# First column group of a squared-ReLU perceptron with one level of block products, and the work around it reordered

## Chip, cores and metric

The kernel runs on one core of one Trainium2 chip. The metric is the device time of one launch in microseconds. All data are fp32; matrix products run on TensorE in fp32, each logical product as two matmul records in the trace.

## What is computed

Two network blocks follow each other on 1024 tokens of width 1024. The change touches the end of the second one: a layer norm, the perceptron with squared ReLU, and the last layer norm.

```python
h = layer_norm_2(ALPHA * h + cross_attention(h, memf, ...), ln2_g, ln2_b)
h = layer_norm_2(ALPHA * h + squared_relu_mlp(h, mlp_w1, mlp_w2), ln3_g, ln3_b)

def squared_relu_mlp(x, w1, w2):          # w1: 1024 x 4096, w2: 4096 x 1024
    hdn = jnp.square(jax.nn.relu(jnp.einsum('bld,df->blf', x, w1)))
    return jnp.einsum('blf,fd->bld', hdn, w2)
```

## The kernel before

Activations lie transposed, features on partitions, tokens in columns; the two halves of 512 tokens are normed one after the other. Norms are numbered: 2 and 3 are the halves of the second layer norm, 4 and 5 those of the third. A norm `n` takes its mean with a matmul by ones over a sum of eight rows (`add_r`, GpSimd), is centred (VectorE), squared (ScalarE), its squares summed (`add_sq` on GpSimd, three of eight on VectorE), and then has its root, its scaling and its shift.

**First product.** The hidden columns are cut into 8 quads of 512. Each quad is a product of a 1024x512 block of `w1` with all tokens, done with the seven products of the Strassen-Winograd scheme; `items` lists these (q, m1), 56 in all, in the order (0,1) (0,2) (1,1) (1,2), then 6 7 5 4 3 of quad 0, the same of quad 1, then quads 2 to 7 with `QUAD_ORDER` 1 2 6 7 5 4 3. The token side of product m1 is an operand (`OPERANDS`: B11, B21, B22 or the sums T1 to T4), made once in quad 0 by `operand`. The weight side is a raw block or one of the sums S1 to S4, made by GpSimd in `level_sums`. Each item is done by the same scheme again (a second level): seven passes of two products of 256 columns, whose weight sums s1 to s4 GpSimd makes (also `level_sums`, in a ring of three items) and whose token sums t1 to t4 come from `more_sums` (called as `more`). TensorE's order over the items is `PASSES`, in which passes 7 and 4 of an item fall into the next item's turn:

```python
PASSES = ((1, 0), (7, -1), (5, 0), (2, 0), (4, -1), (6, 0), (3, 0))
```

Blocks of an item are put together in PSUM and by three VectorE adds (`add_block`: c11, c12, c22) and four ScalarE copies (`copy`: t1, t5, t2, c21). Pass 4 waits for `c22`, pass 6 for `t1`, 3 for `t5`, 7 for `t2`. Then VectorE joins the seven products of a quad (`combine`: U2, C11, U3, U4, C22, C21, C12), squares the ReLU in one op (R11, R22, R21, R12: `max` with 0, then `mult` with itself), and forms the token operands of the second product (T3, T1, T2, T4), which SP stores to DRAM (`store_operand`).

**Second product.** `LastProduct`: 28 steps, seven products m1 in `LAST_ORDER` (5 6 1 7 4 2 3) times four groups g. For step n, `load` fetches the hidden operand and the raw weights, `chain_sum` (VectorE) makes S, `right_sums` (VectorE) and `left_sums` (GpSimd) make the second level's sums, and PE does seven passes of 256 columns. After the last group of an m1 `add_blocks` empties PSUM and `combine_late` joins (U2 to C11) and adds the residual (R22, R21, R11, R12).

Every engine runs its queue in program order, and each of these orders is written out by hand (`copies_order`, `blocks_in_order`, the loops at the end of each engine's block); a wait is a count on one semaphore per engine (`Marks`). Norm 3's steps lie between the first items, norm 4's in steps 25 and 26 of the second product, norm 5's after it.

## Time and profile before

| | |
|---|---|
| median of three runs | 3309.31 us (3306.61 to 3310.32) |
| profiled execution | 3313.49 us, span 3311.7 us |
| first product of the quads to the first of the second product | 2520.2 to 2917.0 us of the span |
| second product | 2917.0 to 3278.0 us |
| last norm and stores | 3278.0 to 3311.7 us |
| busy over the whole span: TensorE, VectorE, GpSimd, ScalarE | 3170.8, 1801.2, 1099.2, 714.4 us |
| mean granted clock of TensorE | 0.98 of 2.4 GHz |

Times in the rows are microseconds from the span's start. PE is TensorE, DVE VectorE, ACT ScalarE, POOL GpSimd, SPq the queue of SyncE. An x behind a row counts records; square brackets give the idle time ahead of the row and what ended it.

### The profile page before, as it was taken

To read this page: it belongs to the slowest core of one execution; us is meant where nothing else is said; L and a number is where in the kernel's file an instruction comes from. 1 tells how busy PE (TensorE), PEld (TensorE's weight loads), DVE (VectorE), ACT (ScalarE), POOL (GpSimd) and SP (SyncE) were. 2 spreads that over 40 slices of the span, in tenths; PEclk is the share of its full clock that TensorE was granted. 3 is DMA by queue.
4 is the path that set the end of the run, shared out by engine and by line. 5 is a ranking of instruction groups with operands and counts; after the bars stand their busy time and mean duration, and the time that the engine had idled before them with its cause. 6 is when DMAs were issued, how large, how long until landed. Compare 5 with 4: busy or idle time off the path is not lost.

```text
span 3311.7 us, 31339 instructions
## 1 busy us (share of the span) xinstructions
PE 3170.8 (96%) x11908; PEld 1854.2 (56%) x11908; DVE 1801.2 (54%) x2603; ACT 714.4 (22%) x1247; POOL 1099.2 (33%) x846
## 2 busy tenths in 40 slices
PE   8989998999999999999999999999998899989995
PEld 3446464864444444444444554544555688878884
DVE  2387976731544343434325654752126777786866
ACT  3333334321100101101212234212223122200002
POOL 0010130003433433331211000341016999945545
PEclk9999999999999999999999999999999899999997
DMA  4211101241111111120212211211112233375651
GB/s 136 73 42 39 51 30 51 79 151 51 39 42 48 38 38 51 44 70 32 83 64 78 64 52 51 77 51 64 51 64 76 83 135 139 119 282 196 217 181 72
DMA packets 185859, 273.72 MB, mean 83 GB/s; under 512 B 7664, under 2 KB 134128, under 8 KB 185200
## 3 DMA queue, kind: packets, MB, share of 16 engines
q1 hardware_dynamic: 185712, 271.72, 24.1%
q8 instruction: 97, 1.59, 0.2%
q14 instruction: 50, 0.41, 0.0%
HBM read 231.85 MB, written 39.85 MB: 82 GB/s over the span
## 4 chain that ended last, share of the span: by engine, by line
PE 83%; DVE 9%; POOL 3%; issue 2%; ACT 2%; DMA 1%; SPq 0%; DVEq 0%; POOLq 0%; ACTq 0%
PE psum L1795 22%; PE psum L181 10%; PE psum L3421 8%; PE psum L3237 8%; PE psum L2320 8%; PE psum L402 7%; PE psum L1836 3%; PE psum L3937 3%; PE psum L1824 2%; DVE arena L1337 2%; DVE arena L1335 2%; PE psum L555 1%; POOL arena L4429 1%; PE psum L3914 1%; PE psum L3875 1%
## 5 line engine op out<-in xcount | busy, mean ns | idle before, releaser
L1795 PE MATMUL psum<-arena 128*128 128x512 f32 x1736 | 746.4, 592 | 1.9 <-DVE arena L2099 1.9
L1795 PEld LDWEIGHTS psum<-arena 128*128 128x128 f32 x1736 | 329.4, 190 | 417.2 <-issue 412.1
L2022 DVE TENSOR_TENSOR arena<-arena,psum 128x512 f32<-128x512 f32 x336 | 221.4, 686 | 458.5 <-PE psum L1795 275.4
L3421 PE MATMUL psum<-arena 128*128 128x256 f32 x1568 | 343.5, 382 | 3.3 <-DVE arena L3458 2.9
L402 PE MATMUL psum<-arena 128*128 128x512 f32 x768 | 336.9, 598 | 4.9 <-DVE arena L1193 4.9
L285 POOL TENSOR_TENSOR arena<-arena 128x512 f32<-128x512 f32 (+1 forms) x190 | 221.4, 1198 | 348.9 <-DMA arena<-w_ffn_gate 165.0
L181 PE MATMUL psum<-arena 128*128 128x512 f32 x768 | 332.4, 592 | 1.5 <-ACT arena L4095 1.5
L3237 PE MATMUL psum<-arena 128*128 128x256 f32 x1244 | 293.9, 390 | 38.3 <-DVE arena L3261 22.8
L3421 PEld LDWEIGHTS psum<-arena 128*128 128x128 f32 x1568 | 300.4, 192 | 46.9 <-issue 4.3
L3237 PEld LDWEIGHTS psum<-arena 128*128 128x128 f32 x1244 | 240.7, 195 | 81.5 <-DVE arena L3261 29.5
L402 PEld LDWEIGHTS psum<-arena 128*128 128x128 f32 x768 | 146.4, 192 | 188.7 <-issue 186.9
L2320 PE MATMUL psum<-arena 128*128 128x512 f32 x576 | 251.4, 595 | 0.0
L181 PEld LDWEIGHTS psum<-arena 128*128 128x128 f32 x768 | 145.8, 190 | 182.1 <-issue 180.6
L2320 PEld LDWEIGHTS psum<-arena 128*128 128x128 f32 x576 | 108.9, 191 | 136.4 <-issue 136.4
L4305 DVE TENSOR_TENSOR arena<-arena 128x1024 f32<-128x1024 f32 x88 | 152.9, 1738 | 0.4
L4429 POOL TENSOR_TENSOR arena<-arena 128x512 f32<-128x512 f32 x75 | 103.6, 1382 | 114.0 <-DVE arena L4179 73.0
L1943 ACT ACTIVATE arena<-psum 128x512 f32<-128x512 f32 x22 | 13.1, 597 | 536.6 <-PE psum L1795 536.6
L3141 POOL TENSOR_TENSOR arena<-small_sb,consts_sb 128x512 f32<-128x512 f32 x16 | 16.2, 1041 | 324.3 <-PE psum L2398 169.6
L2140 POOL TENSOR_TENSOR arena<-arena 128x512 f32<-128x512 f32 x42 | 53.1, 1264 | 194.8 <-ACT arena L1925 194.6
L1836 PE MATMUL psum<-arena 128*128 128x512 f32 x256 | 112.5, 592 | 0.0
L3937 PE MATMUL psum<-arena 128*128 128x512 f32 x224 | 97.0, 593 | 0.9 <-DVEq L241 0.9
L3439 POOL TENSOR_TENSOR arena<-arena 128x512 f32<-128x512 f32 x28 | 42.2, 1509 | 157.5 <-PE psum L3421 54.9
(529 smaller groups left out, 4179.0 us busy)
## 6 DMA issues: line engine op xcount, KB each, us to landing
arena<-w_in SPq DMA_DIRECT2D x42, 1024.0 KB, 5.3
arena<-mlp_w SPq DMA_DIRECT2D x72, 512.0 KB, 6.8
arena<-mlp_w SPq DMA_DIRECT2D x8, 2048.0 KB, 9.2
mlp_hidden_T<-arena SPq DMA_DIRECT2D x32, 512.0 KB, 2.6
arena<-mlp_hidden_T SPq DMA_DIRECT2D x16, 1024.0 KB, 6.0
arena<-w_out SPq DMA_DIRECT2D x12, 1024.0 KB, 5.0
mlp_hidden_B<-arena SPq DMA_DIRECT2D x24, 512.0 KB, 2.7
arena<-mlp_hidden_B SPq DMA_DIRECT2D x12, 1024.0 KB, 5.3
```

The lines of the kernel that those rows point to most:

```text
L181: mm = nc.tensor.matmul(self.out(i, x.shape[1]), part, x, start=(kk == 0), stop=(kk == self.kt - 1))
L285: return g.tensor_tensor(to[:, 0:kn, :], block_of(*a), block_of(*b), op)
L402: mm = nc.tensor.matmul(ps, slot(u)[:, k, m * P:(m + 1) * P], hn(k, h), start=(k == 0), stop=(k == KD - 1))
L1795: mm = nc.tensor.matmul(ps, left, right, start=(k == 0), stop=(k == kn - 1))
L1836: mm = nc.tensor.matmul(ps, raw(v)[:, k, m * P:(m + 1) * P], half_of(env, N0, k, h), start=(k == 0), stop=(k == KD - 1))
L2022: return v_.tensor_tensor(dst, dst, tiles.ps(*key), op)
L2320: mm = nc.tensor.matmul(ps, slot(n)[:, k, m * P:(m + 1) * P], x_half(k, h), start=(k == 0), stop=(k == KD - 1))
L3237: mm = self.env.nc.tensor.matmul(self.ps(n, m), left[:, k, :], right[:, k, :], start=(m in (1, 5, 2) and k == 0), stop=(k == 1), skip_grou ...
L3421: mm = self.env.nc.tensor.matmul(ps[:, 256 * r:256 * r + 256], left[:, s, r * P:(r + 1) * P], right[:, s, :], start=(first and s == 0 and ...
L3937: mm = nc.tensor.matmul(ps, left, mix_right[m](k), start=(k == 0), stop=(k == 3))
L4305: blocks.mark(v_.tensor_tensor(to, one, two, op), name, q)
L4429: fin(pool, nc.gpsimd.tensor_tensor(dst, dst, src, ALU.add), sem, value)
```

## The change

- The seven items of quad 0 are done with one level only: two passes `p0` and `p1` of four products of 512 columns each (`plain_product`), copied out of PSUM by ScalarE (`plain_copy`); no s1 to s4 for them. `passes` puts them between the passes of the two-level items.
- Squared ReLU of the first product moves from VectorE to ScalarE, as a Relu and, after it, a Square, both in place (`squared_relu`), one item later in the order.
- Orders: token sums (`more`) are made later and wait for the last pass of quad 0's item of the same operand; norm 3's rows are taken in another order and its steps sit at other items; on GpSimd `level_sums` runs for items 4, 5, 2, 3, 8, then 9 and on.
- Loads of the second product are split: `load_hidden` and `load_weights`; the weights of step 0 come after quad 6, the hidden operands of steps 0 and 1 before quad 7's `B22` store.
- `chain_sum(0)` goes from behind to ahead of `c22` of item 54, `right_sums(0)` between `c11` and `c12` of item 55, `right_sums(1)` ahead of `chain_sum(1)`.
- Norm sums: `R11` and `R12` come earlier and `C11` after `chain_sum(25)`; `add_r(4)` runs in two parts; `add_r(5)` sums the rows without `F_`, and TensorE adds the four rows of `F_` to the mean itself.

```diff
-def passes(items):
-
-    return [(n + d, m) for n in range(items + 1) for m, d in PASSES if 0 <= n + d < items]
+def passes(items, plain):
+
+    order = []
+    for n in range(items + 1):
+        if n in plain:
+            slots = ((7, -1), ("p0", 0), (4, -1), ("p1", 0))
+        else:
+            slots = PASSES
+        order += [(n + d, m) for m, d in slots if 0 <= n + d < items and (n + d in plain) == (m in ("p0", "p1"))]
+    return order
...
+        self.plain = {n for n, (q, m1) in enumerate(items) if q == 0}
...
+    def plain_product(self, pe, n, m):
+        q, m1 = self.items[n]
+        left, right, rt = self.weights(q, m1), self.x_of(OPERANDS[m1]), int(m == "p1")
+        if m == "p0":
+            if m1 == 1:
+                pe.wait_ge(*self.raw_in(q))
+            elif m1 in (3, 5, 6, 7):
+                self.summed.wait(pe, f"S{ {5: 1, 6: 2, 7: 3, 3: 4}[m1]}", q)
+        self.wait_bank(pe, n, m)
+        b = self.bank_of(n, m)
+        for k in range(4):
+            if m == "p0" and k % 2 == 0:
+                self.need_x(pe, OPERANDS[m1], 1 if k == 0 else 2)
+            mm = self.env.nc.tensor.matmul(self.env.ps(b * BANK, (b + 1) * BANK), left[:, k, rt * P:(rt + 1) * P], right[:, k, :], start=(k == 0),
+                                           stop=(k == 3), skip_group_check=True)
+        self.made.mark(mm, n, m)
+
+    def plain_copy(self, act, n, m):
+        q, m1 = self.items[n]
+        self.made.wait(act, n, m)
+        if m1 == 4:
+            self.blocks.wait(act, "C11", q)
+        b = self.bank_of(n, m)
+        to = self.out(q, m1)[:, int(m == "p1"), :]
+        self.copied.mark(self.env.nc.scalar.activation(to, self.env.ps(b * BANK, (b + 1) * BANK), ACT.Copy), m, n)
...
+            if q:
+                self.made.wait(pool, self.number[q, 6], 4)
...
-    order_in = lambda n: (4, 5, 6, 7, 0, 1, 2, 3) if n == 3 else range(8)
+    order_in = lambda n: (4, 5, 0, 1, 6, 7, 2, 3) if n == 3 else range(8)
...
-        combined = {6: ("U2", "C11", "R11"), 7: ("U3",), 5: ("U4", "C22", "R22"), 4: ("C21", "R21"), 3: ("C12", "R12")}
+        combined = {6: ("U2", "C11"), 7: ("U3",), 5: ("U4", "C22"), 4: ("C21",), 3: ("C12",)}
...
+        first_part = lambda n: 0 if n == 9 else 1
+        late_combined = {5: (), 6: (), 1: ("U2",), 7: ("U3", "U4", "C22", "R22"), 4: ("C21", "R21", "R11"), 2: (), 3: ()}
...
+        sums_first = (4, 5, 2, 3, 8)
+        more_after = {10: "T4", 11: "B22"}
...
+                    pe.wait_ge(scaled, 40)
                 ps = mean(n) if n else early.open(pe, "mean", n)
-                mm = nc.tensor.matmul(ps, env.const["ones"], acc_r(n), start=True, stop=True)
+                mm = nc.tensor.matmul(ps, env.const["ones"], acc_r(n), start=True, stop=(n != 5))
+                if n == 5:
+                    for i in range(4):
+                        blocks.wait(pe, "late", ("d12", "d21")[i // 2], 3)
+                        mm = nc.tensor.matmul(ps, env.const["ones"], F_[:, i, :], start=False, stop=(i == 3))
...
-                    late.load(sp, 0, before_late_load)
+                    late.load_hidden(sp, 0, before_late_load)
+                    late.load_hidden(sp, 1, before_late_load)
                 store_operand("B22", "R22", q)
                 if q == QUADS - 1:
-                    late.load(sp, 1, before_late_load)
-                    late.load(sp, 2, before_late_load)
+                    late.load_weights(sp, 1, before_late_load)
+                    late.load_hidden(sp, 2, before_late_load)
+                    late.load_weights(sp, 2, before_late_load)
                 store_operand("B21", "R21", q)
                 if q + 2 < QUADS:
-                    made.wait(sp, at_item[q, 4], 4)
+                    made.wait(sp, *quads.last_pass(at_item[q, 4]))
                     summed.wait(sp, "S4", q)
                     load_quad(q + 2)
+                elif q + 2 == QUADS:
+                    late.load_weights(sp, 0, before_late_load)
...
+            def squared_relu(n):
+                for name, q in activated_after(n):
+                    to = {"R11": a_[q % 2], "R22": e_, "R21": d_, "R12": c_[q % 2]}[name]
+                    blocks.wait(act, "C" + name[1:], q)
+                    copied.mark(nc.scalar.activation(to, to, ACT.Relu), "relu", name, q)
+                    copied.wait(act, "relu", name, q)
+                    copied.mark(nc.scalar.activation(to, to, ACT.Square), "square", name, q)
+
             for n in range(LAST_N + 1):
+                if n in quads.plain:
+                    quads.plain_copy(act, n, "p0")
+                    if n == 0:
+                        squares(3, range(4))
+                    quads.plain_copy(act, n, "p1")
+                    if n == 0:
+                        squares(3, range(4, 8))
+                    elif n == 1:
+                        std(3)
+                    if two_level(n - 1):
+                        quads.copy(act, n - 1, "c21")
+                    squared_relu(n - 2)
+                    continue
+                if n == 10:
+                    squared_relu(n - 2)
                 if n < LAST_N:
                     quads.copy(act, n, "t1")
-                if n == 1:
-                    squares(3, range(4))
-                if n < LAST_N:
                     quads.copy(act, n, "t5")
-                if n == 2:
-                    std(3)
-                elif n == 3:
-                    shifts(3, range(4))
-                if n:
+                if n == 3:
+                    shifts(3, range(4, 8))
+                if n != 10:
+                    squared_relu(n - 2)
+                if two_level(n - 1):
                     quads.copy(act, n - 1, "c21")
-                if n == 1:
-                    squares(3, range(4, 8))
-                elif n == 3:
-                    shifts(3, range(4, 8))
                 if n < LAST_N:
                     quads.copy(act, n, "t2")
+                if n == 2:
+                    shifts(3, range(4))
+            squared_relu(LAST_N - 1)
...
-                    dve.wait_ge(h_ready, 32)
+                    dve.wait_ge(h_ready, 24 + 4 + 4 * p)
...
+            centre(3)
             for n in range(LAST_N + 1):
-                if n:
+                if two_level(n - 1):
                     quads.add_block(dve, n - 1, "c22")
-                if n == 1:
-                    centre(3, range(4, 8))
-                elif n == LAST_N - 1:
-                    late.chain_sum(dve, 0)
-                elif n == LAST_N:
-                    late.right_sums(dve, 0)
-                    prepare(1)
-                for name, q in combined_after(n - 2)[1:]:
-                    combine(name, q)
-                if n < LAST_N:
-                    quads.add_block(dve, n, "c11")
-                    if n == 2:
-                        invert(3)
-                    elif n == 3:
-                        scale_rows(3, order_in(3)[4:8])
-                    quads.add_block(dve, n, "c12")
-                for name, q in combined_after(n - 1)[:1]:
-                    combine(name, q)
-                if n == 0:
-                    centre(3, range(4))
-                elif n == 2:
-                    scale_rows(3, order_in(3)[0:4])
-                elif n == 3:
+                if n == 3:
                     for p in range(2):
                         operand("T3", p)
                         operand("T2", p)
-                        if p == 0:
-                            operand("T4", p)
+                elif n == 4:
+                    for name in ("T4", "T1"):
+                        for p in range(2):
+                            operand(name, p)
+                elif n == 2:
+                    invert(3)
+                    scale_rows(3, order_in(3)[0:4])
+                for name, q in combined_after(n - 2)[first_part(n - 2):]:
+                    combine(name, q)
...
+                if two_level(n):
+                    quads.add_block(dve, n, "c11")
+                    if n == 2:
+                        scale_rows(3, order_in(3)[4:8])
+                    elif n == LAST_N - 1:
+                        late.right_sums(dve, 0)
+                    quads.add_block(dve, n, "c12")
+                for name, q in combined_after(n - 1)[:first_part(n - 1)]:
+                    combine(name, q)
+                if n == 5:
                     more("T2")
-                elif n == 4:
-                    operand("T1", 0)
-                    operand("T1", 1)
+                elif n == 7:
                     more("T1")
-                    operand("T4", 1)
-            for name, q in combined_after(LAST_N - 1)[1:]:
-                combine(name, q)
+                elif n == LAST_N - 2:
+                    late.chain_sum(dve, 0)
+            late.right_sums(dve, 1)
+            late.chain_sum(dve, 1)
...
-                    prepare(n + 2)
+                    late.chain_sum(dve, n + 2)
+                    if n == 23:
+                        combine_late("C11")
+                    late.right_sums(dve, n + 2)
                 if g == 3:
                     for name in late_combined[m1]:
                         combine_late(name)
+                elif n == 22:
+                    combine_late("R12")
+            blocks.wait(dve, "late", "C12", 1)
...
+                made.wait(pool, *quads.last_pass(at_item[0, {"T3": 7, "T4": 4, "B22": 3}[o]]))
...
-            quads.level_sums(pool, 0)
             pool.wait_ge(pv_done, 16)
-            quads.level_sums(pool, 1)
+            quads.level_sums(pool, 4)
+            quads.level_sums(pool, 5)
             add_r(3, range(5, 8))
             quads.level_sums(pool, 2)
             add_sq(3)
-            for n in range(3, LAST_N):
+            quads.level_sums(pool, 3)
+            quads.level_sums(pool, 8)
+            more("T3")
+            for n in range(9, LAST_N):
                 quads.level_sums(pool, n)
-                if n in (4, 6, 7):
-                    more({4: "T3", 6: "T4", 7: "B22"}[n])
-            for n in range(26):
+                if n in more_after:
+                    more(more_after[n])
+            for n in range(LATE):
+                if n == 26:
+                    add_r(4, range(4))
+                elif n == 27:
+                    add_sq(4)
                 late.left_sums(pool, n)
-            add_r(4, (4, 5, 6, 7, 0, 1, 2, 3))
-            late.left_sums(pool, 26)
-            add_sq(4)
-            late.left_sums(pool, 27)
+                if n == 22:
+                    add_r(4, range(4, 8))
```

## Rows read from the trace of the kernel before

**Rows 1.** Windows of the second half: length, busy (x) by engine, PEclk, DMA share, GB/s

```profile
2520.20:2645.20 125.00, 98.84 (x412) 82.06 (x411) 89.58 (x102) 30.29 (x72) 105.29 (x81) 0.88 0.18 68
2645.20:2901.30 256.10, 250.66 (x1149) 217.17 (x1148) 192.88 (x210) 63.00 (x164) 250.03 (x185) 1.00 0.36 134
2901.30:2917.00 15.70, 8.98 (x38) 7.38 (x37) 12.06 (x12) 1.53 (x4) 7.66 (x4) 0.84 0.50 179
...
3234.60:3278.00 43.40, 33.61 (x154) 28.30 (x154) 32.05 (x36) 10.75 (x18) 29.27 (x22) 0.92 0.13 49
3278.00:3311.70 33.70, 7.71 (x27) 5.77 (x26) 15.28 (x22) 10.27 (x17) 11.58 (x9) 0.54 0.17 62
```

**Rows 2.** What line 3237 (TensorE) waited for: us in all, waits

```profile
  DVE arena L3261: 52.3, 32
```

**Rows 3.** Timeline of TensorE: start, length, work xcount [idle before]

```profile
2404.52 13.90 PE L181 MATMUL psum<-arena 128*128 128x512 f32 x32
...
2607.46 3.78 PE L3237 MATMUL psum<-arena 128*128 128x256 f32 x8 [4.95 <-POOL arena L3280]
...
2640.85 6.21 PE L3237 MATMUL psum<-arena 128*128 128x256 f32 x28
```

**Rows 4.** Groups by line and shape: busy, mean ns | idle before

```profile
L1958 ACT ACTIVATE arena<-arena 128x1024 f32<-128x1024 f32 x22 | 21.9, 1048 | 0.0
...
L1943 ACT ACTIVATE arena<-psum 128x512 f32<-128x512 f32 x22 | 13.1, 597 | 536.6 <-PE psum L1795 536.6
...
L3247 ACT ACTIVATE conformer<-psum 128x256 f32<-128x256 f32 x112 | 43.1, 384 | 183.0 <-PE psum L3237 181.7 <-DVE arena L3261 1.3
...
L4088 ACT ACT_TABLE_LOAD x2 | 2.6, 1283 | 0.0
...
L4299 DVE SCALAR_TENSOR_TENSOR arena<-arena 128x1024 f32<-128x1024 f32 x32 | 52.7, 1648 | 0.6
...
L292 PE MATMUL psum<-consts_sb,arena 128*128 128x1 f32 x16 | 1.8, 245 | 0.0
```

**Rows 5.** Timeline of GpSimd, VectorE and TensorE about one collision, quad 3

```profile
2719.09 2.34 POOL L3287 TENSOR_TENSOR arena<-arena 128x1024 f32<-128x1024 f32 x1
2721.51 1.60 POOL L3292 TENSOR_TENSOR consts_sb<-arena 128x256 f32<-128x256 f32 x1
2723.07 0.72 POOL L3293 TENSOR_TENSOR consts_sb<-arena 128x256 f32<-128x256 f32 x1
...
2719.71 2.80 DVE L4305 TENSOR_TENSOR arena<-arena 128x1024 f32<-128x1024 f32 x1
...
2722.90 2.43 PE L3237 MATMUL psum<-arena 128*128 128x256 f32 x10 [0.33 <-DVE arena L3261]
```

**Rows 6.** Timeline of VectorE and TensorE at the change to the second product

```profile
2901.93 1.22 DVE L4305 TENSOR_TENSOR arena<-arena 128x1024 f32<-128x1024 f32 x1
...
2906.89 2.29 DVE L3458 TENSOR_TENSOR arena<-arena 128x2048 f32<-128x2048 f32 x1 [3.14 <-DMA arena<-mlp_w]
...
2916.32 1.75 DVE L3480 TENSOR_TENSOR arena<-arena 128x512 f32<-128x512 f32 x1
...
2915.11 2.07 PE L3237 MATMUL psum<-arena 128*128 128x256 f32 x4 [6.72 <-DVE arena L3261]
```

**Rows 7.** Timeline of GpSimd and TensorE, last steps and closing norm

```profile
3226.24 16.40 POOL L4429 TENSOR_TENSOR arena<-arena 128x512 f32<-128x512 f32 x7
...
3278.43 6.14 POOL L4429 TENSOR_TENSOR arena<-arena 128x512 f32<-128x512 f32 x4 [9.79 <-DVE arena L4354]
...
3242.70 2.08 PE L3828 MATMUL psum<-arena,consts_sb 128*128 128x512 f32 x2 [8.11 <-POOL arena L4429]
3244.57 11.55 PE L3421 MATMUL psum<-arena 128*128 128x256 f32 x48
...
3263.05 1.16 PE L299 MATMUL psum<-consts_sb,small_sb 128*128 128x128 f32 x8 [1.69 <-DVE small_sb L4208]
...
3284.62 2.07 PE L3828 MATMUL psum<-arena,consts_sb 128*128 128x512 f32 x2 [6.61 <-POOL arena L4429]
```

196 lines of the change are left out of this document (120 added, 76 removed).

## Prediction

> **What bounds the kernel now.** I read the windows of the second half first [rows 1]. Columns after the stretch are its length, then busy time of each engine. TensorE is the chain nearly everywhere; what can be won is where its length exceeds its busy time. Five stretches matter. The first fourteen items of the perceptron's quads take 125.0 us with TensorE busy 98.84 and a granted clock of 0.88. The following 41 items take 256.1 at full clock, GpSimd busy 250.03. The change-over to the second product takes 15.7 with 8.98 busy. The last four steps and their norm take 43.4 with 33.61 busy. The closing norm takes 33.7, almost without TensorE.
>
> Who kept TensorE waiting in the quads: above all the block adds of VectorE (line 3261), 52.3 us in 32 waits [rows 2]. In the first items the gaps are long enough for the clock to fall: after 4.95 us of waiting, eight records took 3.78, while 28 in a stretch took 6.21 [rows 3]. A logical product is two records. With the last record 0.38 long, a record of 256 columns steps by (6.21-0.38)/27 = 0.216; one of 512 columns by (13.90-0.59)/31 = 0.429 [rows 3]. So a pass (two products) of the two-level scheme is 0.864, an item of seven passes 6.05, and an item done plainly (8 products of 512 columns) 16 x 0.429 = 6.87. Each plain item thus costs 0.82 more TensorE work, 5.7 us over seven. The question is how much waiting goes with it.
>
> **First fourteen items.** Work left: seven plain items 48.1; 47 passes of the other items up to pass 3 of item 13, 40.6; the statistics 1.8 [rows 4], about 1.2 [rows 7] and two records of 512 columns, 0.86: 3.8. Together 92.5 us. Now the queues, in us from the stage's start.
> Items 0 and 1 need only `B11` and `B21`, which are there; they fill 0 to 14.7 and hide the norm: mean after 4.3, VectorE's eight centring steps, ScalarE's squares and GpSimd's five sums end near 14. Items 2 and 3 run to about 33, waiting 0.7 for `c22` of item 2 behind the row scaling. `T3` and `T2` (four 128x1024 sums, 1.22 each alone [rows 6]) follow on VectorE from 25.7 to 30.7; item 4 needs the second half of `T2` at 30.9. `T4` and `T1` end by 38, item 6 needs `T1` at 44. Items 4 to 8 need no level sums and are copied by ScalarE (0.60 each [rows 4]) under 3.4 us passes: no wait up to 64.6. So TensorE stays at full clock where it now drops. The moved buffers cost nothing: the same ops on other addresses. Nor do the norm's rows in another order, which let the first halves of `T3` and `T2` start after four shifts; otherwise item 4 would wait some 3 us more.
> Behind that the trouble is moved, not gone. GpSimd's `more("T3")` now waits for item 5's last pass, 43.9, and from there it has eleven blocks of sums to make for items 9 to 13, 36.3 us at the undisturbed 0.72 per 256 columns and 2.34 per 1024 [rows 5]. VectorE's fifteen combinations fall into the same time, and the two hold each other up: an op of 256 columns takes 1.60 beside them [rows 5]. With an idle 1.8 and about 12 of such waits, `S4` of quad 1 is ready near 94, and TensorE wants it near 91.5. On ScalarE, `R22` and `R21` of quad 0 stand ahead of `t1` and `t2` of item 9 (1.3 lost over two items); on VectorE the four operands of quad 0 wait for `R12` and delay `c22` of item 10 (1.5); `U2` and `C11` share one iteration, then `R11` delays `t2` of item 11 (2.5); `s12` is late by about 3.4; 1.0 for the smaller ones. With the 0.7 that is 10: end at 102.5 instead of 125.0, **gain 22.5**. Without GpSimd's and VectorE's mutual waits it would be 97 (28 gained), with full ones 110 (15 gained).
>
> **Squared ReLU on ScalarE, quads 2 to 7.** VectorE loses four ops of 1.648 per quad; ScalarE gains eight. No Relu runs in this half; the nearest row is an in-place 128x1024 activation of 1.048 [rows 4]. With the wait between the steps I take 2.2 per pair (bounds 2.1 and, if each step pays a further copy-sized 0.38, 2.9). ScalarE is 63.0 busy of 256.1, so it fits; what counts is its order. In a period the second combination is ready about 3.5 to 4.4 after the period's start, its pair ends at 5.7 to 6.6, then `c21` and `t2` (0.384 each) end at 6.5 to 7.4, and TensorE wants `t2` at 6.91. Two such periods per quad (`R11`, `R22`), a loss of 0 to 0.5 each. Waiting on ScalarE's pair are also SP's stores and, through `R12`, VectorE's `T3`; both have a period's slack here.
> Against it: these 41 items lose 256.1 - 41 x 6.05 = 8 us now, mostly where a combination stands in GpSimd's way: 2.80 instead of 1.22 beside a weight sum of 2.34, and `c22` behind it stops TensorE for 0.33 [rows 5, 6]. Four fewer such ops per quad give GpSimd some 4 us back, so its weight sums move earlier. I take 3.5 of the 8 back: **gain 3.5** (bounds -5 and +6).
> The Trainium skill speaks against this part (ScalarE: Activation LUTs, Rules for kernel authors): relu and mul belong on VectorE, not ScalarE. By the rows a pair is dearer by about 0.5 us; were all 32 pairs on the path, as the rule would have it, 16 us were lost and the time near 3289. That is the first rival below; no run yet shows which engine's time counts.
>
> **Change-over.** Now `chain_sum(0)` stands behind `c22` of item 54 and waits for weights until 2906.89; TensorE waits 6.72 and runs its next four records in 2.07 [rows 6]. The early `load_weights(0)` removes that wait (the copy is issued a quad earlier and hidden by it). But the sum (2.29 [rows 6]) now stands ahead of `c22` of item 54, which comes at 4.45 of its period instead of 3.46: 1.0 lost. Then `right_sums(0)` stands ahead of `c12` and `c22` of item 55, while GpSimd's `left_sums(0)`, released by the same chain sum, runs against it. Four ops of up to 1.75 [rows 6], with `C22` and `C21` around them, put `c22` at 15.0 and the second product's start at 15.0 + 2.07 = 17.1, against 15.7: **loss 1.4** (without the collisions 13, a gain of 3; with all 1.75 and 2.80 some 20, a loss of 4). The later chain sum 1 has weights at about 20 and is wanted by 28. SP's queue gains no copies: weights 0 (four issues of some 0.6 us) go ahead of quad 6's operand stores, operand 1 ahead of quad 7's `B22` store; both stores are read a step or more later, which hides them; were a store waited for, it would cost those 2.4.
>
> **Norm of the first half.** TensorE waits 8.11 for GpSimd's eight sums, whose last seven took 16.40 because VectorE ran `R11`, `R12` and chain sums beside them; clock and refill cost about 2.2 more (mean 2.07 instead of 0.86 plus 48 records in 11.55 instead of 10.4) [rows 7]. Changed, four sums run two steps earlier and `C11` comes before `right_sums(25)`: the last four end near 3234, when TensorE arrives. The 10.3 are not all kept: GpSimd turns to the squares one `left_sums` later, so the variance waits about 1.9 and the root 3.0 instead of 1.69 [rows 7]: **gain 7.1** (4 to 10).
>
> **Closing norm.** After the last product GpSimd still adds four rows, 6.14, and the mean starts after 6.61 of idle and takes 2.07 [rows 7]: end 8.7 after the last product. Changed, `R12` has put the older part into the sum early, and TensorE adds the four rows of `F_` itself: five logical products of 512 columns, 5 x 0.86 = 4.3, with no idle before them. **Gain 4.3** (3 if they run half at the low clock).
>
> **Sum.** 22.5 + 3.5 - 1.4 + 7.1 + 4.3 = 36.0, against the profiled execution: span 3311.7 gives 3275.7, its time of 3313.49 gives 3277.5. That execution lies 4.2 above the runs' median of 3309.31, so on the runs' scale it is 3273.
>
> **Rivals.** *ScalarE becomes the bound*: from a combination that is ready later than 4.0 into its period, `t2` holds TensorE. At 4.6 it loses 0.7 in 13 periods, 9, and the 3.5 are gone: 3286. For it: `C11` and `C22` run when GpSimd's sums are just released. Against: ScalarE is three quarters idle.
> *GpSimd stays behind after item 8*: mutual waits in full, first items end at 110, 3281. It decides if quad 1's `S4` ends later than 94.
> *The change-over closes too, and quads run clean*: +4.5 and +2.5, mean norm +2: 3264. Against: `left_sums(0)` and `right_sums(0)` start together.
> *Slower*: if Relu and Copy or Square need different activation tables, each pair brings two loads. The trace has loads of 1.283 [rows 4]; in the quads Copy, Square and Identity run without any between them. Then the two late pairs per quad lose 2.6 each and the other two 1.5: 8.2 a quad, 58 over seven, 3331. It decides at the first load in this stage. The Trainium skill (ScalarE: Activation LUTs, Table sets) holds that relu and copy are filler in every set; by that this rival is void, and no run here shows it.
>
> **From this the numbers.** Forecast as summed (3267 to 3279) 0.58; GpSimd behind 0.14; ScalarE bound 0.11; cleaner than summed 0.12; table loads 0.03; nothing gained 0.02. The range runs from the clean case's lower bounds, 3261, to the ScalarE case with the transfer of 4 us lost at the change-over, 3290. A measurement of this kernel tells about 0.2% from no change, 7 us: faster 0.95, same 0.01, slower 0.04.
>
> **What would show it.** The first fourteen items (start of the quads to pass 3 of item 13) should take 98 to 107 us at clock near 1, with the remaining waits after item 8; the 41 items behind 249 to 256; no idle over 1 us ahead of the first half's mean; the last mean within 4.5 us of the last product; an idle of 5 to 8 us at the change-over. Wrong would be: idle of TensorE put down to ScalarE in every quad, table loads among the pairs, waits in items 4 to 8 (an operand or a residual store I took as hidden), or a stall at the second product's later steps, where `R11` and `R12` now stand ahead of right sums.

## The result, and the profile after

The changed kernel takes 3268.53 us (median of four runs, 3265.43 to 3273.68), the kernel before 3309.12 in the runs beside them: ratio 0.9876, 95% interval 0.9864 to 0.9889. Forecast were 3273 and a range of 3261 to 3290. The profiled execution took 3273.68, its span is 3271.8, so the sum to hold against the forecast 36.0 is 3311.7 - 3271.8 = 39.9. Windows of the changed kernel, cut at the same places as [rows 1] (length, busy by engine, granted clock, DMA), with the stretch of the second layer that [rows 1] leaves out:

```profile
2520.80:2622.20 101.40, 94.84 (x328) 60.59 (x327) 65.58 (x71) 38.92 (x70) 70.81 (x54) 0.98 0.22 83
2622.20:2876.90 254.70, 249.97 (x1150) 217.37 (x1149) 145.59 (x187) 106.02 (x211) 222.09 (x190) 1.00 0.38 142
2876.90:2892.80 15.90, 9.41 (x37) 7.21 (x36) 13.71 (x13) 5.55 (x8) 6.75 (x4) 0.87 0.52 181
2892.80:3206.30 313.50, 312.80 (x1442) 274.47 (x1441) 238.42 (x175) 6.08 (x9) 177.57 (x109) 1.00 0.62 218
3206.30:3242.00 35.70, 34.68 (x155) 29.77 (x154) 26.09 (x32) 10.76 (x18) 26.51 (x21) 0.90 0.16 60
3242.00:3271.80 29.80, 10.10 (x35) 6.99 (x34) 14.83 (x22) 10.27 (x17) 5.69 (x5) 0.64 0.19 71
```

| stretch | forecast gain | before | after | gain |
|---|---|---|---|---|
| start to the first item | 0 | 2520.2 | 2520.8 | -0.6 |
| first fourteen items | 22.5 | 125.0 | 101.4 | 23.6 |
| 41 items | 3.5 | 256.1 | 254.7 | 1.4 |
| change-over | -1.4 | 15.7 | 15.9 | -0.2 |
| second layer up to the mean of the first half | 0 | 3234.6 - 2917.0 = 317.6 | 313.5 | 4.1 |
| last steps, norm of the first half | 7.1 | 43.4 | 35.7 | 7.7 |
| closing norm | 4.3 | 33.7 | 29.8 | 3.9 |

What the products of the two-level scheme waited for (the view of [rows 2], which counts the weight load and the product of one wait each):

```profile
  DVE arena L3306: 15.4, 13
  POOL arena L3349: 9.1, 5
...
  ACT small_sb L3298: 3.0, 1
```

Block adds fell from 52.3 to 15.4; new is line 3349, GpSimd's sum s4. The same view also lists who waited for these products. GpSimd's lines of it, first in the changed kernel (L3328 makes S2, L3344 makes s1), then in the kernel before (L3292 makes s1):

```profile
  POOL arena L3328: 10.7, 4
  POOL arena L3344: 10.1, 5
...
  POOL consts_sb L3344: 4.4, 2
```

```profile
  POOL consts_sb L3292: 1.2, 1
```

So GpSimd, which had 1.6 us of such waits before (0.4 of them ahead of S2), now waits 25.2 us for TensorE. All of that lies in the 41 items, where it was busy for 250.03 us and now is for 222.09.

One place where TensorE waits for s4, quad 4, in the timelines of GpSimd, VectorE and TensorE, then the durations (min/median/max ns) of GpSimd's S4 and of ScalarE's Relu (its Square has the same median):

```profile
2712.21 2.36 POOL L3328 TENSOR_TENSOR arena<-arena 128x1024 f32<-128x1024 f32 x1 [2.68 <-PE psum L3261]
...
2733.13 3.35 POOL L3336 TENSOR_TENSOR arena<-arena 128x1024 f32<-128x1024 f32 x1
...
2739.61 0.72 POOL L3349 TENSOR_TENSOR arena<-arena 128x256 f32<-128x256 f32 x1
...
2732.55 1.72 DVE L4427 TENSOR_TENSOR arena<-arena 128x1024 f32<-128x1024 f32 x1
...
2734.53 3.04 DVE L4427 TENSOR_TENSOR arena<-arena 128x1024 f32<-128x1024 f32 x1
...
2740.43 1.10 PE L3261 MATMUL psum<-arena 128*128 128x256 f32 x4 [1.54 <-POOL arena L3349]
```

```profile
L3336 POOL TENSOR_TENSOR arena<-arena x8: 2346/3334/3406, 2536.5 to 2867.2; 128x1024 f32<-128x1024 f32 x8
...
L4255 ACT ACTIVATE arena<-arena x32: 1047/1057/1059, 2572.3 to 2894.8; 128x1024 f32<-128x1024 f32 x32
```

GpSimd waits 2.68 for TensorE ahead of S2, and from there to s4 it runs without a gap. S4 ends at 2736.5 and s4 of the same item at 2740.3; TensorE idles 1.54 for it. S4 shares its time with two VectorE sums. In [rows 5] it took 2.34, near its median there of 2.35; now its median is 3.33. The Trainium skill (SBUF — State Buffer, Who interferes with whom) says that a VectorE instruction with two inputs in SBUF and a GpSimd one that reads SBUF exclude each other, the later one standing until the first has ended. The row agrees: the sum of 3.04 ends at 2737.57, 1.09 behind S4, near its 1.22 alone.

The change-over (VectorE, ScalarE, TensorE) and the norms (TensorE) in the timeline:

```profile
2878.63 2.28 DVE L3513 TENSOR_TENSOR arena<-arena 128x2048 f32<-128x2048 f32 x1
...
2883.59 1.43 DVE L3534 TENSOR_TENSOR arena<-arena 128x512 f32<-128x512 f32 x1
...
2884.46 1.06 ACT L4257 ACTIVATE arena<-arena 128x1024 f32<-128x1024 f32 x1
...
2885.69 0.38 ACT L3298 ACTIVATE small_sb<-psum 128x256 f32<-128x256 f32 x1
...
2881.30 2.86 PE L3261 MATMUL psum<-arena 128*128 128x256 f32 x12 [0.80 <-DVE arena L3306]
2886.21 1.10 PE L3261 MATMUL psum<-arena 128*128 128x256 f32 x4 [2.05 <-POOL arena L3497]
2890.95 2.07 PE L3261 MATMUL psum<-arena 128*128 128x256 f32 x4 [3.64 <-DVE arena L3306]
```

```profile
3206.26 1.02 PE L3918 MATMUL psum<-arena,consts_sb 128*128 128x512 f32 x2
...
3220.92 6.57 PE L3476 MATMUL psum<-arena 128*128 128x256 f32 x16
...
3242.03 1.02 PE L3918 MATMUL psum<-arena,consts_sb 128*128 128x512 f32 x2
3242.89 3.60 PE L3922 MATMUL psum<-arena,consts_sb 128*128 128x512 f32 x8
```

The 6.7 of [rows 6] are split into 0.80, 2.05 and 3.64. The first and the last are waits for c22, behind the chain sum (line 3513) and the right sums (3534). The 2.05 is put down to GpSimd's sum for the second product (line 3497), but that pass, number 7 of item 55, waits for s3 and t2 of its own item. GpSimd's s3 was done at 2872.1. The copy t2 ended at 2886.07, just ahead of the pass; it stood behind the Relu and Square of C22, which VectorE had ended at 2883.33. So this wait is ScalarE's. Both means start without the idle of 8.11 and 6.61 of [rows 7].

### The profile page after: what moved, and what is told of

Its sections match the earlier page's. It is cut to its first block, busy times and chain, and to the rows that moved or that the text cites. A ratio compares the mean times of both kernels' runs of the same rounds, so it can differ in the third digit from the quotient of the medians.

```text
span 3271.8 us, 31100 instructions
## 1 busy us (share of the span) xinstructions
PE 3169.1 (97%) x11832; PEld 1835.1 (56%) x11832; DVE 1732.8 (53%) x2550; ACT 772.4 (24%) x1297; POOL 1036.3 (32%) x818
## 4 chain that ended last, share of the span: by engine, by line
PE 84%; DVE 8%; POOL 4%; ACT 2%; issue 1%; DMA 0%; SPq 0%; DVEq 0%; POOLq 0%; ACTq 0%
PE psum L1795 22%; PE psum L181 10%; PE psum L3476 9%; PE psum L2320 8%; PE psum L402 7%; PE psum L3261 6%; PE psum L1836 3%; PE psum L4031 3%; PE psum L1824 2%; DVE arena L1337 2%; DVE arena L1335 2%; PE psum L3278 1%; PE psum L555 1%; PE psum L4008 1%; PE psum L3969 1%
## 5 line engine op out<-in xcount | busy, mean ns | idle before, releaser
L1795 PEld LDWEIGHTS psum<-arena 128*128 128x128 f32 x1736 | 329.4, 190 | 417.2 <-issue 412.1
L3476 PE MATMUL psum<-arena 128*128 128x256 f32 x1568 | 344.0, 382 | 0.7 <-POOL arena L3497 0.7
L3476 PEld LDWEIGHTS psum<-arena 128*128 128x128 f32 x1568 | 300.8, 192 | 43.6 <-POOL arena L3497 1.5
L3261 PE MATMUL psum<-arena 128*128 128x256 f32 x1080 | 247.6, 382 | 15.8 <-DVE arena L3306 7.1
L402 PEld LDWEIGHTS psum<-arena 128*128 128x128 f32 x768 | 146.6, 192 | 188.9 <-issue 187.1
L181 PEld LDWEIGHTS psum<-arena 128*128 128x128 f32 x768 | 145.8, 190 | 182.1 <-issue 180.6
L3261 PEld LDWEIGHTS psum<-arena 128*128 128x128 f32 x1080 | 204.9, 191 | 49.4 <-DVE arena L3306 8.4
L2320 PEld LDWEIGHTS psum<-arena 128*128 128x128 f32 x576 | 108.9, 190 | 136.4 <-issue 136.4
L4427 DVE TENSOR_TENSOR arena<-arena 128x1024 f32<-128x1024 f32 x88 | 142.6, 1620 | 13.4 <-ACT arena L3289 8.4
```

The source lines that it names most:

```text
L181: mm = nc.tensor.matmul(self.out(i, x.shape[1]), part, x, start=(kk == 0), stop=(kk == self.kt - 1))
L402: mm = nc.tensor.matmul(ps, slot(u)[:, k, m * P:(m + 1) * P], hn(k, h), start=(k == 0), stop=(k == KD - 1))
L1795: mm = nc.tensor.matmul(ps, left, right, start=(k == 0), stop=(k == kn - 1))
L2320: mm = nc.tensor.matmul(ps, slot(n)[:, k, m * P:(m + 1) * P], x_half(k, h), start=(k == 0), stop=(k == KD - 1))
L3261: mm = self.env.nc.tensor.matmul(self.ps(n, m), left[:, k, :], right[:, k, :], start=(m in (1, 5, 2) and k == 0), stop=(k == 1), skip_grou ...
L3476: mm = self.env.nc.tensor.matmul(ps[:, 256 * r:256 * r + 256], left[:, s, r * P:(r + 1) * P], right[:, s, :], start=(first and s == 0 and ...
```

## The experiments

Ahead of the first item the kernels below (but for no_plain) have the changed kernel's instructions, yet that item starts anywhere from 2513.6 to 2520.8 us. So stages are compared, from one profiled execution each; the ratios beside them come from four to five runs. A: start of the first item to the last block of item 13, its c22 (end of the VectorE row); B: to the first pass of the second layer; C: to the start of the mean of the first half; D: to that of the second half; E: to the end of the span. All are differences of two starts or ends in the timelines.

| kernel | A | B | C | D | E | sum | ratio to before, interval |
|---|---|---|---|---|---|---|---|
| before | 127.4 | 269.4 | 325.7 | 41.9 | 27.1 | 791.5 | |
| changed | 103.8 | 268.2 | 313.5 | 35.8 | 29.8 | 751.0 | 0.9876 (0.9864 to 0.9889) |
| after_again | 104.3 | 267.4 | 313.9 | 35.8 | 29.8 | 751.2 | 0.9880 (0.9863 to 0.9896) |
| no_plain | 128.4 | 265.1 | 312.7 | 35.8 | 29.6 | 771.5 | 0.9934 (0.9921 to 0.9946) |
| relu_back | 109.1 | 272.2 | 314.0 | 35.0 | 29.8 | 760.1 | 0.9898 (0.9883 to 0.9913) |
| relu_behind | 104.2 | 269.6 | 313.4 | 36.6 | 29.8 | 753.6 | 0.9873 (0.9860 to 0.9887) |
| s4_vector | 103.6 | 263.1 | 312.4 | 35.8 | 29.5 | 744.4 | 0.9862 (0.9847 to 0.9877) |
| changeover | 104.3 | 262.0 | 315.8 | 35.7 | 29.8 | 747.6 | 0.9862 (0.9846 to 0.9879) |
| loads_undo | 105.8 | 271.6 | 311.3 | 35.8 | 29.9 | 754.3 | 0.9893 (0.9880 to 0.9907) |
| relu_loads_undo | 109.0 | 275.7 | 313.4 | 35.0 | 29.8 | 762.9 | 0.9903 (0.9890 to 0.9917) |
| loads_order_undo | 104.3 | 272.4 | 316.3 | 35.8 | 29.8 | 758.5 | 0.9897 (0.9881 to 0.9914) |
| norm4_undo | 105.7 | 271.5 | 322.7 | 35.2 | 29.5 | 764.5 | 0.9910 (0.9895 to 0.9925) |
| norm5_undo | 104.2 | 267.6 | 314.4 | 41.8 | 27.5 | 755.5 | 0.9885 (0.9871 to 0.9898) |
| best | 103.7 | 258.6 | 314.3 | 35.0 | 29.5 | 741.1 | 0.9840 (0.9826 to 0.9855) |

**after_again.**

> The changed kernel once more, unaltered, as the yardstick of the runs beside it on the same chip. Every theory expects the 3268.5 us of its first runs within 2 us, and in its profile the same stages: the first fourteen products in 101.4 us, the 41 after them in 254.7, the change-over to the second layer in 16.0.

It came out within 1 us in each stage; its median of 3271.72 is 3.2 above the first one, where 2 were expected. Where a kernel's stage is not touched, A differs by up to 2 us and B by up to 4 from here: norm4_undo, unchanged up to there, waits for s4 in five quads in place of three, and in A it idles as long as here (6.5) at a granted clock of 0.97 in place of 0.98. Of the intervals in the table only those of no_plain and best lie clear of both of the changed kernel's. For the others the trace has to show the cause. C differs by up to 1.5 where the second layer is not touched.

**no_plain**: quad 0 in two levels.

```diff
-        self.plain = {n for n, (q, m1) in enumerate(items) if q == 0}
+        self.plain = set()
...
+            quads.level_sums(pool, 0)
             pool.wait_ge(pv_done, 16)
-            quads.level_sums(pool, 4)
-            quads.level_sums(pool, 5)
+            quads.level_sums(pool, 1)
...
```

> The changed kernel with the seven products of the first column group in block products of two levels again, and VectorE's, ScalarE's and GpSimd's orders around the first fourteen products as they were before the change; squared ReLU on ScalarE, order of loads, chain sum and norm sums stay changed. Theory 1 (the plain products carry the gain of the first group): the first fourteen products take 120 to 127 us in place of 101.4, the rest stays within 2 us, and the run is 19 to 26 us slower than the changed kernel. Theory 2 (VectorE and the port that it shares with GpSimd carry it, by the squared ReLU that left): 115 us or less, and the run is 13 us slower at most. Theory 3 (the plain products gain more than they show, since they also set GpSimd ahead in the later groups): the 41 products after them also get 3 us or more longer.

A is 24 us longer, all that the first group had gained; theory 2 is out, theory 3 too (B is rather shorter). The whole run is 20 us longer by the stages and 14 to 18 by the medians (3286.13), where theory 1 has 19 to 26. The plain products and the orders around them went together; which of the two carries how much stays open. The waits of TensorE are back, two of them (issue: the view names no engine):

```profile
2553.67 2.05 PE L3261 MATMUL psum<-arena 128*128 128x256 f32 x4 [5.34 <-issue]
...
2577.86 6.36 PE L3261 MATMUL psum<-arena 128*128 128x256 f32 x20 [5.99 <-DVE arena L3306]
```

**relu_back**: squared ReLU on VectorE.

```diff
-        combined = {6: ("U2", "C11"), 7: ("U3",), 5: ("U4", "C22"), 4: ("C21",), 3: ("C12",)}
+        combined = {6: ("U2", "C11", "R11"), 7: ("U3",), 5: ("U4", "C22", "R22"), 4: ("C21", "R21"), 3: ("C12", "R12")}
...
-            return [("R" + name[1:], q) for name, q in combined_after(n) if name[0] == "C"]
+            return []
...
+                if name[0] == "R":
+                    to = {"R11": a, "R22": e, "R21": d, "R12": c}[name]
+                    blocks.mark(v_.scalar_tensor_tensor(to, to, 0.0, to, ALU.max, ALU.mult), name, q)
+                    return
```

> The changed kernel with the squared ReLU back on VectorE, one operation of 1.65 us right behind each C, and none on ScalarE; all else as it was. Theory 1 (taking 32 x 1.65 us from VectorE is worth a few us): the wait of about 3 us for the chain sum of the second layer's first products comes back, and in the column groups waits of 1 us for c22 come beside those for s4: 5 to 9 us slower than the changed kernel. Theory 2 (the move is hidden, all is gained elsewhere): within 2 us of it. Theory 3 (two passes of 1.06 us on ScalarE hold its copies back more than VectorE did): 2 to 6 us faster than the changed kernel, and the wait of 2.96 us of the twelfth product is gone.

Theory 1 has the size (5 by the medians of that set, where all four runs lie above all four of after_again; 9 by the stages), but not the places. C did not change, so the second layer's wait has another cause. A grew by 5, to 109.1; it is 109.0 in relu_loads_undo, which has the same ReLU, and 103.6 to 105.8 in the kernels with plain items and the ReLU on ScalarE. B grew by 4 to 5, no more than untouched kernels differ by. TensorE's timeline:

```profile
2596.68 7.89 PE L3261 MATMUL psum<-arena 128*128 128x256 f32 x28 [5.16 <-POOL arena L3344]
2608.48 2.07 PE L3261 MATMUL psum<-arena,consts_sb 128*128 128x256 f32 x4 [3.91 <-POOL consts_sb L3344]
...
2684.11 1.99 PE L3261 MATMUL psum<-arena 128*128 128x256 f32 x8 [0.96 <-POOL arena L3331]
...
2894.18 2.07 PE L3261 MATMUL psum<-arena 128*128 128x256 f32 x4 [7.04 <-DVE arena L3306]
```

It is GpSimd that comes late (s1 in items 11 and 12, S3 in six quads) when VectorE has these four operations more. It no longer waits for TensorE: in the 41 items it is busy for 253.50 of 259.10 us. Up to the change-over the waits in B are 6.3 in place of 4.7, for S3 and c22 where they were for s4; in the change-over they are 8.4 (the 7.04 is one of them) in place of 6.5. S4 keeps its median of 3.33, so the squared ReLU's move is not what made it longer. The rule named in the prediction, relu on VectorE (Trainium skill, ScalarE: Activation LUTs, Rules for kernel authors), doesn't carry over to this kernel, where VectorE's operations stand in GpSimd's way: the pair costs 2.11 on ScalarE, VectorE's one operation 1.65 [rows 4], and the kernel with the dearer one is faster. No table load stands among the pairs, as the Trainium skill (ScalarE: Activation LUTs, Table sets) states for Relu and Copy.

**relu_behind**: the pair behind the copy t2.

```diff
-                if n != 10:
-                    squared_relu(n - 2)
                 if two_level(n - 1):
                     quads.copy(act, n - 1, "c21")
                 if n < LAST_N:
                     quads.copy(act, n, "t2")
+                if n != 10:
+                    squared_relu(n - 2)
```

> The changed kernel with ScalarE's Relu and Square of a block behind the copy t2 of the product, in place of ahead of c21 and t2; all else as it was. Theory 1 (the pair of 2.12 us ahead of t2 makes the wait of 2.96 us in the twelfth product): that wait falls under 1 us, the first fourteen products take 101 to 102 us up to their last block in place of 104, and the run is 2 to 3 us faster than the changed kernel. Theory 2 (the pair then holds back t1 and t5 of the next product instead): waits of 0.5 us or more for t1 or t5 appear in the column groups, and the time is the same within 1 us or longer.

Theory 1 fell. The wait of 2.96 went, and 3.29 for GpSimd took its place (TensorE, then GpSimd):

```profile
2604.73 2.07 PE L3261 MATMUL psum<-arena,consts_sb 128*128 128x256 f32 x4 [3.29 <-POOL consts_sb L3344]
...
2601.87 2.12 POOL L3364 TENSOR_TENSOR arena<-arena 128x512 f32<-128x512 f32 x1
2603.96 0.72 POOL L3344 TENSOR_TENSOR consts_sb<-arena 128x256 f32<-128x256 f32 x1
```

Token sums (line 3364), 2.12 beside VectorE, hold s1 back. Two engines were late there by about the same; the profile had named the later one. Theory 2 has the time right, but none of its waits of 0.5 for t1 or t5 came. In quads 2 to 7 no wait for s4 is left, since S4's median fell back to 2.35. But nine waits for c22, 4.7 us in sum, stand in place of the 4.5 for s4, and B stays. At the place of the first timeline (VectorE, then TensorE) it is now VectorE's sum that takes long beside S4:

```profile
2729.55 3.39 DVE L4429 TENSOR_TENSOR arena<-arena 128x1024 f32<-128x1024 f32 x1
...
2733.32 4.58 PE L3261 MATMUL psum<-arena 128*128 128x256 f32 x20 [0.89 <-DVE arena L3306]
```

In the change-over the 2.05 for t2 is gone too, and the wait for c22 grew from 3.64 to 5.93.

**s4_vector**: S4 on VectorE.

```diff
+    def weight_sum(self, dve, q):
+        s = self.levels[1]
+        self.summed.wait(dve, "s4", self.number[q, 6])
+        self.made.wait(dve, self.number[q, 6], 4)
+        self.blocks.mark(self.env.nc.vector.tensor_tensor(s, self.raw(q)[:, 4:8, 0:256], s, ALU.subtract), "S4", q)
...
+                    if items[n][1] == 7 and items[n][0]:
+                        quads.weight_sum(dve, items[n][0])
                     quads.add_block(dve, n, "c12")
```

> The changed kernel with the large weight sum S4 of column groups 1 to 7 on VectorE, between the blocks c11 and c12 of product seven, in place of GpSimd; all else as it was. Theory 1 (GpSimd is the late one in the column groups): the wait of 1.5 us for s4 that stands once in groups 4 to 6 is gone, GpSimd is 3.4 us earlier at product three, and the 41 products take 249 to 251 us in place of 254.7: 4 to 5 us less than the changed kernel. Theory 2 (VectorE is as full as GpSimd): S4 of 1.2 to 3 us pushes c12 and c22 of product seven, TensorE waits there 1 to 2 us in each of seven groups, and the time stays the same or gets up to 8 us longer.

Theory 1: no wait for s4 is left, B is 4 to 5 us shorter and below that of every other kernel but changeover and best (265.1 to 275.7). All four runs lie below all four of after_again beside them (3260.70 to 3266.31 against 3268.06 to 3272.89), though the intervals of the ratios overlap. S4's durations on VectorE, and a window from item 14 on in the columns of the first fence:

```profile
L3356 DVE TENSOR_TENSOR arena<-arena x7: 1231/1690/1708, 2595.4 to 2851.6; 128x1024 f32<-128x1024 f32 x7
```

```profile
2618.00:2865.00 247.00, 246.54 (x1137) 214.95 (x1136) 148.79 (x190) 106.00 (x209) 205.84 (x180) 1.00 0.38 144
```

TensorE is busy for 246.54 of 247.00 there.

**changeover**: two sums of the second layer moved, and C21 of the last quad behind them.

```diff
-        first_part = lambda n: 0 if n == 9 else 1
+        first_part = lambda n: 0 if n in (9, LAST_N - 2) else 1
...
-                    elif n == LAST_N - 1:
-                        late.right_sums(dve, 0)
+                    elif n == LAST_N - 2:
+                        late.chain_sum(dve, 0)
                     quads.add_block(dve, n, "c12")
...
                     quads.add_block(dve, n - 1, "c22")
+                if n == LAST_N:
+                    late.right_sums(dve, 0)
```

> The changed kernel with two sums of the second layer elsewhere in VectorE's order: the chain sum of its first item between the blocks c11 and c12 of the last product but one (VectorE is idle there for 2.14 us), its four operand sums behind the last block c22, and C21 behind them. Theory 1 (VectorE's order sets the change-over): the three waits of TensorE, 0.80, 2.05 and 3.64 us, fall to one of about 0.7, the change-over comes down from 16.0 to about 10.5 us, and the run takes 5 to 6 us less than the changed kernel. Theory 2 (the loads of the second layer set it): the waits stay 6 us in sum and are put down to DMA, and the time stays within 1 us. Theory 3 (the sums only move their wait): passes five to seven of the second layer's first item wait 3 us or more for t2, and 2 us or less are gained.

The change-over took 2886.86 - 2876.36 = 10.5, as theory 1 has it, but only 3.5 of the 5 to 6 us stay in the sum, and the interval of the whole run overlaps the changed kernel's. TensorE:

```profile
2884.20 1.10 PE L3261 MATMUL psum<-arena 128*128 128x256 f32 x4 [1.63 <-ACT small_sb L3298]
...
2904.76 7.57 PE L3476 MATMUL psum<-arena 128*128 128x256 f32 x26 [2.20 <-POOL arena L3497]
```

2.20 are given back at once: GpSimd's sums of the second layer's item 1 wait for its chain sum, which stands behind its right sums. Whether that order is the reason is not shown: best, below, turns it round, and as much waiting stays.

**The 4.1 us of the second layer.** In the kernel before, VectorE and TensorE show there:

```profile
2925.17 2.29 DVE L3458 TENSOR_TENSOR arena<-arena 128x2048 f32<-128x2048 f32 x1 [5.78 <-DMA arena<-mlp_w]
...
2945.20 162.65 PE L3421 MATMUL psum<-arena 128*128 128x256 f32 x744 [2.91 <-DVE arena L3458]
```

The chain sum of item 1 waits 5.78 for its weights with everything else of VectorE behind it, so that of item 2, which starts at 2942.77, is late by 2.91. Three kernels asked which part removed this. **loads_undo**:

```diff
                     late.load_hidden(sp, 0, before_late_load)
-                    late.load_hidden(sp, 1, before_late_load)
+                    late.load_weights(sp, 0, before_late_load)
...
-                elif q + 2 == QUADS:
-                    late.load_weights(sp, 0, before_late_load)
```

> The changed kernel with the order of the second layer's first loads on the DMA queue as before the change: operand and weights of items 0 and 1 each together, the weights of item 0 behind the operand of item 0 in the last group. Theory 1 (the loads' order took the wait of 2.9 us for the third chain sum out of the second layer, for with the squared ReLU back on VectorE that wait did not return): VectorE's chain sum of item 1 waits 3 us or more for DMA, passes of items 1 to 2 wait 2 to 4 us, and the run is 2 to 6 us slower than the changed kernel. Theory 2 (the places of chain sum and right sums on VectorE did it): within 1 us of the changed kernel from the first product to the mean of the first half.

Theory 1 fell: C is even shorter. The loads show at the change-over instead, where the first chain sum waits (VectorE, TensorE):

```profile
2881.05 2.29 DVE L3513 TENSOR_TENSOR arena<-arena 128x2048 f32<-128x2048 f32 x1 [4.42 <-DMA arena<-mlp_w]
...
2883.73 6.01 PE L3261 MATMUL psum<-arena 128*128 128x256 f32 x16 [5.31 <-DVE arena L3306]
```

**relu_loads_undo**, the edits of relu_back and loads_undo together:

> The changed kernel with two parts undone at once: squared ReLU on VectorE, and the order of the second layer's first loads as before the change. With one of them undone the second layer took 312 to 314 us from its first pass to the mean of the first half, as in the changed kernel (before: 317.6 by the same rows of the page, in part for a wait of 2.91 us for the chain sum of item 2). Theory 1 (the wait needs both, a late load ahead and the squared ReLU behind it on VectorE): the wait of 2 us or more returns, and this stretch takes 316 to 318 us. Theory 2 (it came from VectorE's order of chain sums and right sums, which stays changed here): no such wait, 312 to 314 us.

Theory 2: C stays 313.4. That left VectorE's order. **loads_order_undo** has that order as before, together with the loads of loads_undo (here the part on VectorE):

```diff
+                elif n == LAST_N:
+                    late.right_sums(dve, 0)
+                    late.chain_sum(dve, 1)
+                    late.right_sums(dve, 1)
...
-            late.right_sums(dve, 1)
-            late.chain_sum(dve, 1)
```

> The changed kernel with the second layer's first loads and VectorE's order around them as before the change: operand and weights of items 0 and 1 each together, the first chain sum behind the block c22 of the last product but one, and the second one, behind the last c22, between the right sums of items 0 and 1. Squared ReLU stays on ScalarE. Theory 1 (the second chain sum, which waits for its weights with all else of VectorE behind it, made the wait in the second layer): the chain sum of item 1 waits 3 us or more for DMA, a wait of 2 us or more stands in items 1 to 3, and the second layer takes 316 to 318 us from its first pass to the mean of the first half, in place of 313.5. Theory 2 (it also takes the squared ReLU on VectorE): the chain sum waits, but the stretch stays at 312 to 314 us.

```profile
2899.10 2.29 DVE L3513 TENSOR_TENSOR arena<-arena 128x2048 f32<-128x2048 f32 x1 [6.82 <-DMA arena<-mlp_w]
...
2918.86 3.69 PE L3476 MATMUL psum<-arena 128*128 128x256 f32 x16 [2.12 <-DVE arena L3513]
```

Theory 1: the wait is back without the squared ReLU on VectorE, and C is 316.3. In the changed kernel a chain sum that waits for a DMA no longer stands ahead of right sums that need none: that is worth 2.4 to 2.8 of the 4.1. The rest has no cause shown. The new order suffices with the loads as before (loads_undo); no kernel asked whether the new loads alone would have done, but in best, below, a chain sum put ahead again waits 5.31 in spite of them.

**norm4_undo** and **norm5_undo**: the two norms' sums as before.

```diff
-        late_combined = {5: (), 6: (), 1: ("U2",), 7: ("U3", "U4", "C22", "R22"), 4: ("C21", "R21", "R11"), 2: (), 3: ()}
+        late_combined = {5: (), 6: (), 1: ("U2",), 7: ("U3", "U4", "C22", "R22"), 4: ("C21", "R21"), 2: ("C11", "R11", "R12"), 3: ()}
...
-                    add_r(4, range(4))
+                    add_r(4, (4, 5, 6, 7, 0, 1, 2, 3))
```

> The changed kernel with the norm of the first half fed as before the change: C11, R11 and R12 behind the last block of step two, and GpSimd's eight row sums ahead of its block sums of item 26 in one run. Theory 1 (the row sums were what the mean waited for): the mean waits 7 to 8 us again, the stretch from it to the mean of the second half takes 42 to 44 us in place of 35.8, and the run is 7 to 8 us slower than the changed kernel. Theory 2 (GpSimd has become faster since VectorE leaves the port alone there): the mean waits 4 us or less, and the run is 2 to 4 us slower.

```diff
-                if n == 5:
-                    for i in range(4):
-                        blocks.wait(pe, "late", ("d12", "d21")[i // 2], 3)
-                        mm = nc.tensor.matmul(ps, env.const["ones"], F_[:, i, :], start=False, stop=(i == 3))
```

> The changed kernel with the closing norm's mean as one product over sums that hold every row: GpSimd's last four row sums wait for the finished rows of C12, and the four products with the rows of the last step are gone. Theory 1 (these products stand for GpSimd's late row sums): the mean waits 6 to 7 us, the time from it to the end is 3.5 to 4.5 us longer, and so is the run. Theory 2 (the four products of 0.43 us each and the wait of VectorE eat most of it): 0 to 2 us slower.

Both as theory 1 has it: C and D together grow by 8.1 to 8.6, D and E by 3.7. The waits of TensorE, first half and second half:

```profile
3216.75 2.07 PE L3916 MATMUL psum<-arena,consts_sb 128*128 128x512 f32 x2 [8.11 <-POOL arena L4544]
```

```profile
3242.52 2.08 PE L3918 MATMUL psum<-arena,consts_sb 128*128 128x512 f32 x2 [6.60 <-POOL arena L4545]
```

The medians alone show no loss for norm5_undo (3271.04). In its profiled execution, of 3271.80, the first item starts at 2514.5, 4.6 earlier than in after_again, which hides the loss there; whether it did in the other runs no trace shows.

**best**: the edits of s4_vector, changeover and relu_behind, and

```diff
+            late.chain_sum(dve, 1)
             late.right_sums(dve, 1)
-            late.chain_sum(dve, 1)
```

> The changed kernel with four things in another order: S4 on VectorE, the chain sum and right sums of the second layer's first item where VectorE idles, its second chain sum ahead of the second right sums, and ScalarE's Relu and Square behind t2. If the waits are independent the gains add: 4 to 5 us for S4, 5 to 6 for the change-over with the wait of 2.20 us that the chain sum of the second item left behind, 2 to 3 for t2: 11 to 14 us less than the changed kernel, about 3258 us. If S4 and the chain sum fill the same idle time of VectorE, or the later squared ReLU delays the operands of the second layer, 6 us or less.

3259.57 us, ratio 0.9840 (0.9826 to 0.9855), below the changed kernel's interval: some 10 us less by the stages, just under the 11 to 14 expected. S4 and change-over add up in B (9 us), relu_behind adds nothing, as by itself, and 2.2 of waiting stay in the second layer. Its last edit puts the second chain sum ahead again, and that sum waits for its weights with all of VectorE behind it, though the loads come in the new order (VectorE, then TensorE):

```profile
2888.00 2.29 DVE L3520 TENSOR_TENSOR arena<-arena 128x2048 f32<-128x2048 f32 x1 [5.31 <-DMA arena<-mlp_w]
...
2895.41 4.80 PE L3483 MATMUL psum<-arena 128*128 128x256 f32 x21 [0.92 <-POOL arena L3504]
2909.22 145.31 PE L3483 MATMUL psum<-arena 128*128 128x256 f32 x672 [1.28 <-POOL arena L3504]
```

## Why the prediction was right, and where it was off

**First fourteen items** (22.5, measured 23.6): the mechanism was right, and the sum came closer than its terms. Items 0 to 8 end 64.5 us after the start (forecast 64.6) with one wait of 0.56; behind them stand waits of 0.49, 0.66, 1.88 and 2.96, the last at item 11, where 2.5 were expected:

```profile
2609.45 2.04 PE L3261 MATMUL psum<-arena 128*128 128x256 f32 x4 [2.96 <-ACT small_sb L3298]
```

That is 6.6 us of waiting of the 10 forecast. TensorE's own work came to 94.8 in place of 92.5, so the two errors cancel but for 1.1, which is luck. Part of the 2.3 is the clock, granted 0.98 in this stage: the four records of the row took 2.04, while four such records elsewhere take 1.03. no_plain shows that the plain items and the orders around them carry the gain. But relu_back shows that they do so in full only with squared ReLU off VectorE: 3 to 5 of the 23.6 are lost without it, some 3 as waiting (9.6 in place of 6.6) and the rest at a clock of 0.95. The forecast gave the ReLU no part in this stage.

**Squared ReLU, quads 2 to 7** (3.5, measured 1.4): mis-sized, and the step that failed is "four fewer such ops per quad give GpSimd some 4 us back, so its weight sums move earlier". Its first half came true: GpSimd's busy time fell by 27.9 us in the 41 items. The second half did not. 25.2 us of it went into GpSimd's waiting for TensorE to free buffers, ahead of S2 and s1, so it could not run ahead, and its sums behind such a wait still came late. VectorE's c22 did stop holding TensorE, but s4 came 1.5 late in three quads, behind an S4 of 3.33 in place of 2.35. Why S4 now takes the longer turn in the collision stays open: it does so with the ReLU back on VectorE as well, and not in relu_behind, where VectorE's sum takes it. s4_vector takes just these waits away.

**Change-over** (-1.4, measured -0.2): the early loads did remove the wait for weights, and three waits of 6.5 us stand in place of one of 6.7. The first is the 1.0 forecast for the chain sum ahead of c22 (0.80); c22 of item 55 ended 14.0 us into the stretch, where 15.0 was forecast. The 2.05 for ScalarE's t2 was in no term; it did not set the length, since without it, in relu_behind, the waits are 6.7. changeover shows that in the changed kernel VectorE's order, not the loads, sets its length.

**Second layer** (0, measured 4.1): the step that is missing. The forecast asked of the chain sum of item 1 only whether it would now come too late, and not what its place before had cost. The row of 5.78 us of VectorE waiting for DMA stood in the trace of before. Undoing its new place together with the new loads loses 2.4 to 2.8 of the 4.1 again.

**Norms** (7.1 and 4.3, measured 7.7 and 3.9): right. The root's wait of 3.0 didn't come, but 16 records that took 6.57 did: the granted clock was 0.83 in the short column products ahead of them and 0.55 over these records; 16 such records otherwise take about 16 x 0.216 = 3.5.

**Rivals.** ScalarE becoming the bound: TensorE waited for it twice, 2.96 in item 11 and 2.05 in the change-over, and relu_behind, which takes both away, shows another engine late at both places. GpSimd behind after item 8: to a small part, 1.15 us. Table loads: none. The error of the whole, 3.9 by the spans, is as large as the second layer's 4.1; the other errors, up to 2.1 each, cancel.

## What to carry to other kernels

Where two engines stand in each other's way, price an operation by what it does to the other engine: squared ReLU got dearer by 0.5 us a piece on ScalarE and the kernel was 5 to 9 us faster. Time given back to an engine counts only as far as the engine can use it: ask what it would wait for next. Put an operation that waits for a DMA behind those of its engine that don't. When one engine's wait is taken away, look who comes second at the same place, and test it alone: removing one of two waits that end together gains nothing. Check the engine that a view names against what the program waits for there.

## What the runs showed of the hardware

Relu and Square in place took 1.057 us each on 128x1024, with no table load between them. The same S4 took 2.35 to 3.41 us on GpSimd and 1.23 to 1.71 on VectorE (s4_vector); the time depended on what ran beside it. With equal instructions the first item started 7 us apart between profiled executions; why is open.
